# Folding the first two chunks of a down product: seven block products for eight

## The reference, cut to what matters

```
D_MODEL = 1024; D_FF = 2816
def _swiglu(h, w_in, w_out):
    a, b = jnp.split(h @ w_in, 2, axis=-1)
    return (jax.nn.silu(a) * b) @ w_out          # "up" product, then "down" product
...
xl = xl + ml[5] * _swiglu(_modulate(_rmsnorm(xl, norm_g[l, 1]), ml[3], ml[4]), w_ffn_in[l], w_ffn_out[l])
xc = xc + mc[5] * _swiglu(_modulate(_rmsnorm(xc, norm_g[l, 1]), mc[3], mc[4]), w_ffn_in[l], w_ffn_out[l])
```

## Time and profile before

| what | us |
|---|---|
| median of three runs (lowest, highest) | 3171.95 (3167.01, 3172.81) |
| the profiled execution, device time | 3168.27 |
| its span in the trace | 3166.2 |
| TensorE busy in the span | 3006.0 |
| VectorE busy in the span | 1620.0 |
| down product of layer 0, from and to (its last latent step) | 1281.45 to 1435.55 |

### The profile page before, as it was taken

How to read it: one execution, slowest core, us unless ns; L and a number is a source line. 1 busy time by engine, 2 the same in 40 slices (tenths; PEclk the granted TensorE clock), 3 DMA queues, 4 the chain that set the end, 5 groups by cost and what they waited for, 6 DMA issues and landing times. The chain is left out here.

```text
span 3166.2 us, 33940 instructions
## 1 busy us (share of the span) xinstructions
PE 3006.0 (95%) x12718; PEld 2115.9 (67%) x12718; DVE 1620.0 (51%) x3605; ACT 815.2 (26%) x1892; POOL 351.5 (11%) x391
## 2 busy tenths in 40 slices
PE   8999999999999999998999999999999999988776
PEld 3666556758888888586776678888888744443222
DVE  3233454367773676413234447624226587777774
ACT  2222244321002100012122440010023354544443
POOL 0000000010000000100000000000000254433442
PEclk9999999999999999999999999999999999999999
DMA  6212111144442454643322224479533799999997
GB/s 242 87 60 66 54 54 53 54 148 137 125 136 67 147 156 132 205 138 107 107 76 65 73 93 157 148 256 319 197 117 96 268 415 420 420 421 420 420 417 316
DMA packets 280913, 584.86 MB, mean 185 GB/s; under 512 B 11752, under 2 KB 231784, under 8 KB 244400
## 3 DMA queue, kind: packets, MB, share of 16 engines
q0 software_dynamic: 51504, 338.98, 27.2%
q1 hardware_dynamic: 229248, 243.73, 23.9%
HBM read 581.58 MB, written 1.08 MB: 184 GB/s over the span
## 5 line engine op out<-in xcount | busy, mean ns | idle before, releaser
L815 PE MATMUL banks<-normed,weight_ring 128*128 128x512 f32 (+1 forms) x1280 | 484.4, 533 | 12.8 <-PEq L322 12.4
L815 PEld LDWEIGHTS banks<-normed,weight_ring 128*128 128x128 f32 x1280 | 242.7, 191 | 232.7 <-issue 221.8
L824 PE MATMUL banks<-weight_ring,normed 128*128 128x256 f32 x1408 | 318.8, 381 | 0.0
L3710 PE MATMUL banks<-weight_ring,work 128*128 128x512 f32 x512 | 251.7, 616 | 55.1 <-ACT work L3572 54.0
L824 PEld LDWEIGHTS banks<-weight_ring,normed 128*128 128x128 f32 x1408 | 263.8, 190 | 53.5 <-issue 19.4
L3710 PE MATMUL banks<-work 128*128 128x512 f32 x512 | 251.1, 613 | 41.0 <-ACT work L3572 38.8
L436 DVE CUSTOM_DVE_ANT_0 work<-work 128x1024 f32<-128x1024 f32 x176 | 209.2, 1223 | 114.4 <-DMA work<-ada_turned 52.6
L2164 PE MATMUL banks<-normed,weight_ring 128*128 128x256 f32 x1088 | 239.0, 383 | 6.6 <-ACT normed L2364 3.8
L2164 PEld LDWEIGHTS banks<-normed,weight_ring 128*128 128x128 f32 x1088 | 208.9, 192 | 36.2 <-ACT normed L2364 4.2
L1660 PE MATMUL banks<-branches,weight_ring 128*128 128x256 f32 (+1 forms) x656 | 209.2, 481 | 3.4 <-PEq L322 3.4
L3710 PEld LDWEIGHTS banks<-weight_ring,work 128*128 128x128 f32 x512 | 88.6, 191 | 166.3 <-ACT work L3572 102.5
(11 more groups left out here) (558 smaller groups left out, 3952.6 us busy)
## 6 DMA issues: line engine op xcount, KB each, us to landing
weight_ring<-w_in SPq DMA_DIRECT2D x98, 1024.0 KB, 5.3
weight_ring<-w_ffn_in SPq DMA_DIRECT2D x44, 1024.0 KB, 5.4
work<-ada_turned POOLq DMA_DIRECT2D x80, 512.0 KB, 3.8
work<-ada_turned POOLq DMA_DIRECT2D x16, 1536.0 KB, 9.1
weight_ring<-w_ffn_out SPq DMA_DIRECT2D x20, 1024.0 KB, 5.3
weight_ring<-w_out SPq DMA_DIRECT2D x12, 1024.0 KB, 5.4
weight_ring<-w_br_ml SPq DMA_DIRECT2D x8, 1024.0 KB, 5.2
weight_ring<-w_br_da SPq DMA_DIRECT2D x8, 1024.0 KB, 5.4
```

Source lines behind the costliest of these rows:

```text
L815: last = pe.matmul(proj_bank(tile)[:, since:T], w[:, kk, half * P:(half + 1) * P], c.h[:, kk, since:T], start=kk == 0, stop=kk == KT - 1)
L824: last = pe.matmul(proj_bank(tile)[:, x * CHUNK:(x + 1) * CHUNK], c.h[:, kk, j * P:(j + 1) * P], w[:, kk, :], start=kk == 0, stop=kk == KT ...
L3710: last = pe.matmul(c.banks[2 * t + half][:], diag[:, r, :], vrows[r][:, half * 512:(half + 1) * 512], start=e == t * H * K, stop=e == (t + ...
```

## The change

Steps 0 and 1 of the down product are computed in the folded form, over the three cuts in turn with the partial sums left in four PSUM banks. Seven times 11 matmuls of 256 tokens take the place of 44 of 512 tokens in each. VectorE gets a mixture of the weights for each of the six cuts (`mix_cut`) and mixtures of the tokens for the 11 pairs of input tiles: six pairs one at a time behind the up chunks, four pairs together and the last one behind the last up chunk. It also unfolds both products into `spare` and adds them from there (`add_folded`). The modulation tiles are dealt out anew, 5, 5, 6 and 5 between these steps; their number stays 21. The plain steps use other PSUM banks, and the squares of steps 0 and 1 are both summed behind step 2.

```diff
-    BEFORE_OUT, BEFORE_DOWN, DOWN_FIRST = 32, 59, 12
+    BEFORE_OUT, BEFORE_DOWN, DOWN_FIRST = 32, 59, 10
+    FOLDED_DOWN, EARLY_PAIRS, LATE_PAIRS = 2, 6, 4
...
-    B_OUT, B_SUMS, B_UP, B_DOWN = 0, KT, KT + 2, 4
+    B_OUT, B_SUMS, B_UP, B_DOWN = 0, KT, KT + 2, 0
...
+            def folded_down(d):
+
+                n = len(folded) + d
+                first, second, third, fourth = (c.banks[4 * (n % 2) + i] for i in range(4))
+                pe.wait_ge(c.folded_copied, n - 1)
+                for cut, (k0, nk) in enumerate(cuts):
+                    w, pairs = weights(W_DOWN + d * len(cuts) + cut)[:, 0:nk], range(k0 // 2, (k0 + nk) // 2)
+                    mixed = weight_sums[:, mixed_number(d, cut) % 2]
+                    opens, closes = cut == 0, cut == len(cuts) - 1
...
+                    pe.wait_ge(c.fed, pairs[-1] + 1)
+                    done(one(first, 0, their(0, 0), tokens(0, 0), True, True))
+                    if opens:
+                        pe.wait_ge(c.folded_read, 4 * (n - 2) + 1)
+                    one(second, 0, their(1, 0), tokens(1, 0), True, False)
+                    pe.wait_ge(c.weights_mixed, mixed_number(d, cut) + 1)
+                    pe.wait_ge(c.tokens_mixed, 4 + pairs[-1] + 1)
+                    done(one(second, 1, mixture(1), token_mixture(1), False, True))
...
+                    if not closes:
+                        last.then_inc(c.slot_used, 1)
...
+            for d in range(FOLDED_DOWN):
+                folded_down(d)
             for s, (chunk, p0, p1) in enumerate(down_steps):
+                if s < FOLDED_DOWN:
+                    continue
...
-                if s:
-                    sums(down_steps, s - 1, wide * KT, B_SUMS_2)
+                if s == FOLDED_DOWN:
+                    pe.wait_ge(c.folded_read, 4 * (len(folded) + FOLDED_DOWN))
+                    sums(down_steps, 0, wide * KT, B_SUMS_2)
+                sums(down_steps, s - 1, wide * KT, B_SUMS_2)
...
+            def mix_cut(d, cut):
+
+                m, number, nk = mixed_number(d, cut), W_DOWN + d * len(cuts) + cut, cuts[cut][1]
+                out = weight_sums[:, m % 2, :, 0:nk // 2]
+                wait_weights(dve, number)
+                w = c.ring[:, number % SLOTS, 0:nk]
+                if m - 2 < len(folded):
+                    dve.wait_ge(c.folded_product, 4 * (m - 1))
+                else:
+                    wait_cut(dve, *divmod(m - 2 - len(folded), len(cuts)))
+                chain.mark(dve.tensor_tensor(out[:, 0], part_of(w, 0, 1), part_of(w, 1, 1), ALU.add))
+                chain(dve.tensor_tensor(out[:, 2], part_of(w, 0, 0), part_of(w, 0, 1), ALU.subtract))
+                chain(dve.tensor_tensor(out[:, 1], out[:, 0], part_of(w, 0, 0), ALU.subtract))
+                chain(dve.tensor_tensor(out[:, 3], part_of(w, 1, 0), out[:, 1], ALU.subtract))
+                dve.sem_inc(c.weights_mixed, 1)
...
                 if n + 1 < len(folded):
                     mix_weights(n + 1)
+                else:
+                    mix_cut(0, 0)
                 condition(2 if i == 0 else 1)
                 unfold(n)
                 if i:
                     feed(n, chunk)
+                if i and chunk < EARLY_PAIRS:
+                    mix_tokens(ffn[:, 2 * chunk:2 * chunk + 2, :], down_sums(chunk))
+            late = EARLY_PAIRS + LATE_PAIRS
+            mix_tokens(ffn[:, 2 * EARLY_PAIRS:2 * late, :],
+                       c.work[:, SUMS_AT:SUMS_AT + LATE_PAIRS * 4 * NCTX].rearrange("p (k s t) -> p s k t", s=4, k=LATE_PAIRS),
+                       LATE_PAIRS)
+            mix_tokens(ffn[:, 2 * late:NF, :], down_sums(late))
+            mix_cut(0, 1)
 
             assert taken == BEFORE_DOWN
             scales(mod_next, KT, c.vector("norm_g", 2 * KT, 3 * KT))
-            for s in range(len(down_steps)):
-                if s < 2:
-                    condition(DOWN_FIRST if s == 0 else 9)
-                add(down_steps, s, P_DOWN, D_DOWN, B_DOWN, 5 * KT)
+            condition(5)
+            mix_cut(0, 2)
+            condition(DOWN_FIRST - 5)
+            mix_cut(1, 0)
+            unfold(len(folded))
+            add_folded(0)
+            mix_cut(1, 1)
+            condition(6)
+            mix_cut(1, 2)
+            condition(5)
+            unfold(len(folded) + 1)
+            add_folded(1)
+            for s in range(FOLDED_DOWN, len(down_steps)):
+                add(down_steps, s, P_DOWN - 2 * FOLDED_DOWN, D_DOWN, B_DOWN, 5 * KT)
...
```

More of the change, by code:

```diff
@@ L1569, in tail_of_all, with down_sums, mixed_number, wait_cut @@
     D_DOWN = wide * KT
-    B_OUT, B_SUMS, B_UP, B_DOWN = 0, KT, KT + 2, 4
+    B_OUT, B_SUMS, B_UP, B_DOWN = 0, KT, KT + 2, 0
     B_SUMS_2 = B_DOWN + KT
+    def down_sums(pair):
+        if pair < 4:
+            its = c.mg[:, 2 * pair:2 * pair + 2, :].rearrange("p k t -> p (k t)")
+        elif pair == 4:
+            its = gates[1]
+        elif pair == 5:
+            its = c.big[:, NF:NF + 2, :].rearrange("p k t -> p (k t)")
+        elif pair < EARLY_PAIRS + LATE_PAIRS:
+            at = SUMS_AT + (pair - EARLY_PAIRS) * 4 * NCTX
+            its = c.work[:, at:at + 4 * NCTX]
+        else:
+            its = c.h[:, 4:6, :].rearrange("p k t -> p (k t)")
+        return its.rearrange("p (s k t) -> p s k t", s=4, k=1)
+    def mixed_number(d, cut):
+        return len(folded) + d * len(cuts) + cut
+    def wait_cut(engine, d, cut):
+        if cut == len(cuts) - 1:
+            engine.wait_ge(c.folded_product, 4 * (len(folded) + d + 1))
+        else:
+            engine.wait_ge(c.slot_used, d * (len(cuts) - 1) + cut + 1)
     def weight_of(n):
@@ L1598, in target_of @@
     def target_of(n):
+        if n >= len(folded):
+            return spare
         kind, i, chunk = folded[n]
@@ L1635, in wait_used @@
                     s, _, cut = down[n - W_DOWN]
-                    if cut == len(cuts) - 1:
-                        sp.wait_ge(c.product, P_DOWN + 2 * (s + 1))
+                    if s < FOLDED_DOWN:
+                        wait_cut(sp, s, cut)
+                    elif cut == len(cuts) - 1:
+                        sp.wait_ge(c.product, P_DOWN + 2 * (s - FOLDED_DOWN + 1))
                     else:
@@ L1713, in folded_product, with one, their, mixture @@
                 one(fourth, 1, their(1, 1), token_mixture(3)).then_inc(c.folded_product, 1)
+            def folded_down(d):
[6 more added lines that the diff above has]
+                    opens, closes = cut == 0, cut == len(cuts) - 1
+                    def one(out, half, left, right, first_of_bank, last_of_bank):
+                        for k, pair in enumerate(pairs):
+                            last = pe.matmul(out[:, half * NCTX:(half + 1) * NCTX], left(k), right(pair),
+                                             start=opens and first_of_bank and k == 0,
+                                             stop=closes and last_of_bank and k == len(pairs) - 1)
+                        return last
+                    def their(inputs, outputs):
+                        return lambda k: part_of(w, inputs, outputs)[:, k]
+                    def mixture(i):
+                        return lambda k: mixed[:, i, k]
+                    def tokens(inputs, half):
+                        return lambda pair: quarter(ffn, 2 * pair + inputs, half)
+                    def token_mixture(i):
+                        return lambda pair: down_sums(pair)[:, i, 0]
+                    def done(last):
+                        if closes:
+                            last.then_inc(c.folded_product, 1)
+                    pe.wait_ge(c.fed, pairs[-1] + 1)
[6 more added lines that the diff above has]
+                    done(one(second, 1, mixture(1), token_mixture(1), False, True))
+                    if opens:
+                        pe.wait_ge(c.folded_read, 4 * (n - 2) + 3)
+                    one(third, 0, mixture(0), token_mixture(0), True, False)
+                    done(one(third, 1, mixture(2), token_mixture(2), False, True))
+                    if opens:
+                        pe.wait_ge(c.folded_read, 4 * (n - 2) + 4)
+                    one(fourth, 0, mixture(3), tokens(1, 1), True, False)
+                    last = one(fourth, 1, their(1, 1), token_mixture(3), False, True)
+                    done(last)
+                    if not closes:
+                        last.then_inc(c.slot_used, 1)
@@ L1776, in _ @@
                         if cut == 0 and p0 == 0:
-                            pe.wait_ge(c.folded_read, 4 * (len(folded) - (2 if t < 4 else 1) + 1))
+                            pe.wait_ge(c.folded_read, 4 * (len(folded) + 1))
                         elif cut == 0:
@@ L1803, in condition, with mix_tokens @@
                     next(conditioning)
-            def mix_tokens(source, out):
+            def mix_tokens(source, out, count=1):
                 def half(inputs, tokens):
@@ L1813, in mix_tokens @@
```

(13 more changed lines are left out.)

4 lines of the change are left out of this document (2 added, 2 removed).

## The result

The changed kernel takes 3180.72 us (median of 10 runs, 3174.83 to 3185.56), the kernel before 3172.36 us (10 runs, 3167.01 to 3180.21). The ratio is 1.0023, with a 95% interval of 1.0012 to 1.0033, so the change costs about 7.3 us (8.4 by the two medians). The forecast was 3174.8, within 0.2% of no change, and that did not come true: 3180.72 lies above the 3178.3 that the forecast had set as the border to slower. It is inside the range by 0.3 us only, where rival B had put it (3180.6).

A forecast was written before the change was run, and what follows sets the result against it. TensorE bounds the kernel, but would wait for VectorE's mixtures behind modulation tiles: -9.0 + 1.8 + 7.4 + 1.8 + 0.8 = +2.8 us on the median 3171.95, giving 3174.8 us; range 3166.0 to 3181.0.

The forecast's parts named there:

- rival B: Down product: the three tile groups come at their worst, 14.4 + 15.3 + 18.4 us; +8.7 us, 3180.6; chance 0.16.
- matmuls saved: TensorE, down steps 0 and 1: 77 folded matmuls take 33.25 instead of 37.77 us per chunk; -9.0 us for both.
- wait for (0,2): TensorE in chunk 0 asks for this cut's weight mixture at 1308.2, ready at 1310.0; 1.8 us.
- wait for (1,0): TensorE at chunk 1's first cut asks for its mixture at 1319.9, ready at 1327.3; 7.4 us.
- slow clock behind it: TensorE at 1.2 GHz after a long gap: 1.8 us extra behind the wait for (1,0), none behind the wait for (1,2).
- wait for (1,2): TensorE at chunk 1's last cut asks for its mixture at 1352.5, ready at 1353.3; 0.8 us.
- The work beside the up chunks: VectorE's small token mixtures and the mixture of cut (0,0), covered by its waits for TensorE; priced at nothing.
- The first two groups of tiles: VectorE, five modulation tiles each ahead of cuts (0,2) and (1,0): 14.0 us (bounds 12.0, 14.4) and 14.4 (12.0 to 15.3).
- The third group: VectorE, six modulation tiles ahead of the mixture of cut (1,2): 15.8 us (14.25 to 18.4), weight load at its third tile.
- The mixture of (1,1): VectorE's weight mixture for a cut of 8 k in chunk 1: four operations of 0.69 us, 2.75 us in all.
- The clock's price: TensorE's lower level of 1.2 GHz after gaps of 2.28 us or more: about 1.8 us extra; nearly none after 1.82 us.
- The turns of the DMA queues: Equal turns would make a tile load behind a weight load take 5.0 us, not 6.15; sum then about -0.7 us.

The follow-up runs named there:

- the run with tiles late: Changed kernel with VectorE making each mixture as early as possible and nine modulation tiles moved behind the add of chunk 1; 3164.03 us, ratio 0.9975 against the kernel before.
- the control: The changed kernel run once more, nothing altered, beside the kernel before on the same chip; 3181.45 against 3172.28 us, ratio 1.0033.
- the probe: Kernel before, TensorE made to wait for VectorE ahead of steps 2 to 5; 0.1 us extra behind gaps of 1.29 and 2.57 us, total time not used.
- the run with small loads: Changed kernel in its own order, 20 of 21 tile loads of the down product cut to 64 of 1024 columns; 3162.52 us, a single run.

## Why the prediction was right and wrong

The forecast had the mechanism, the place of each gap and their order, and was too low by 5.7 us in the profile. Step by step, in us:

| step | forecast | changed kernel |
|---|---|---|
| matmuls saved | -9.0 | -9.06 (the run with tiles late) |
| wait for (0,2) | 1.8 | 1.98 |
| wait for (1,0) | 7.4 | 7.05 |
| slow clock behind it | 1.8 | 2.9 |
| wait for (1,2) | 0.8 | 3.25 |
| slow clock behind it | 0 | 1.75 |
| drain at three gaps | 0 | 0.5 |
| sum | +2.8 | +8.4 (measured +8.47) |

**The work beside the up chunks** was priced at nothing, rightly. The stage times don't show it, since they begin behind it; the timeline of TensorE does: from 700 us to the first matmul of the down product it is busy without a gap in both kernels (581.45 of 581.45 us before, 584.20 of 584.20 in the changed kernel).

**The first two groups of tiles** were taken at 14.0 and 14.4 us and took 13.9 and 14.0. Reading them as groups from the trace of before, collision included, worked.

**The third group** is the term that was mis-sized: 15.8 us forecast, 18.2 measured (17.2 in the control, from 1340.98 to 1358.21). Its bound of 18.4, tiles 13 to 18 of before, was nearer, though not the same case: there GpSimd's pair adds at 1320.83 held a tile load back by about 0.8 us, to 1322.98, while here they were over before the group began. The weight load fell on the load of the fourth tile, not on the third. The forecast's own times put it there too: cut (1,0) ends at 1337.8, and the fourth tile's load is issued some 3.1 us after the group begins at 1335.3.

```profile
1342.09 0.37 SPq L1678 DMA_DIRECT2D weight_ring<-w_ffn_out  x1
```

```profile
1335.79 1.90 POOL L2175 TENSOR_TENSOR normed<-normed 128x256 f32<-128x256 f32 x2 [7.63 <-ACT normed L2111]
...
1342.31 0.53 POOL L406 DMA_DIRECT2D work<-ada_turned  x1 [0.92 <-DVEq L442]
```

The load issued at 1342.31 was usable at 1350.99, 8.7 us later, not the 6.15 that I had taken from the earlier trace rows as the worst.

**The mixture of (1,1)** took 3.7 us (1335.29 to 1338.97) in place of 2.75. Two of its operations ran 1.22 and 1.09 us instead of 0.69 while GpSimd's pair add at 1335.79 was at work. The forecast counted pair adds for the sums of squares only, not beside a mixture. Every run of the folded form shows the same two long operations; the mixtures of 512 elements with no pair add beside them keep 0.69 us.

These two, less the 1.1 us by which the longer slow stretch held TensorE itself back, put the third wait at 3.25 instead of 0.8 us, which carried it over the point where the clock has a price. Rival B had that course: it said gaps of 2.2, 8.4 and 3.5 us and +8.7. But B took all three groups at their worst, and only the third one was. That its sum is so near is partly luck: the second gap was 1.35 us shorter than B's and the two slow stretches together 1.05 us longer. That the range held the result is luck too, since it ended at B's time. B's chance of 0.16 was too low, since one bad group and a pair add beside a mixture were enough for its outcome.

**The clock's price** was taken as 1.8 us for every gap of 2.28 us or more. The size is not one number: 1.6 to 3.2 us in the nine cases of these runs. The lower point was off as well inside a run of dense matmuls: 2.57 us cost nothing in the probe, though 2.28 us did at the start of another stage. That row was no match: ahead of its gap TensorE ran small matmuls, and the granted clock was already 0.68 from 2328 to 2331 us.

**The turns of the DMA queues.** The Trainium skill, "DMA: Bandwidth & Descriptors", Queues, rings and completion order, says that each DMA engine takes turns between its queues, packet by packet. I read from it that a small load would slip in between the packets of a weight load. Where both queues have packets, the trace agrees: from 1345 to 1350 us of the changed kernel the tile loads (q0, GpSimd's queue) and the weight load (q1, SyncE's) move side by side. The columns are packets, MB and the time that the packets took, as a share of 16 engines' time:

```profile
q0 software_dynamic: 240, 0.88, 47.8%
q1 hardware_dynamic: 618, 0.62, 39.8%
```

The delay stands ahead of that. By the packet records, the first packet of a lone load comes 1.23 us (0.5 MB, issued at 1285.62 in the kernel before) or 1.25 us (32 KB, issued at 1301.94 in the run with small loads) after its issue. Behind a weight load it comes 3.58 us after the issue at 1296.42 and 2.52 us after the issue at 1330.19. In between, only the weight load moves: q1 is the one queue with packets from 1296.8 to 1299.9 in the kernel before, and from 1330.2 to 1332.4 in the run with small loads:

```profile
q1 hardware_dynamic: 918, 0.94, 91.7%
```

```profile
q1 hardware_dynamic: 803, 0.82, 107.7%
```

For the load of 0.5 MB this is the whole 2.35 us: from its first packet to its landing it takes as long as the lone one. For the small load it is 1.27 of the 3.03 us, and another 1.4 us pass between the last two of its 16 landings (1333.83 and 1335.22). So the reading by turns priced a part of the load that was not the slow one. What keeps the first packet back, no run here shows.

**Still open.** The run-to-run spread of the changed kernel (3174.83 to 3185.56) is wider than these causes show in two profiles. The third gap, with its own length and the clock's price behind it, explains some 3 us of it; the rest isn't settled.

## What to carry to other kernels

When an engine that had slack becomes the maker of operands, give it a schedule by due times: here each mixture's due time is a fixed number of matmuls after the cut begins, and work that waits for DMA belongs behind it, not in front. Sum an in-order engine's row with its DMA waits in, group by group, and take each group from the stretch of the trace that has the same neighbours. Leave room even then: the third group took 18.2 and 17.2 us in two profiles of the same kernel. Seven block products for eight saved nothing until the row was reordered; the reordering turned +0.23% into -0.25%.

## What the hardware showed that I had not expected

A VectorE operation with two inputs in SBUF slows down beside a GpSimd add: 1.22 and 1.09 us against 0.69 for 512 elements, and the two adds take 1.90 against 1.40 us. It can fall on GpSimd alone: in the kernel before the tile at 1320.54 kept its 1.23 us, and the two pair adds beside it took 2.21. The Trainium skill, "GPSIMD Engine Reference", 1. Specifications, says that the two engines share their SBUF interfaces and get in each other's way when VectorE has two SBUF inputs; the trace agrees, with the numbers just given.

A tile load of 32 KB is held up by a 1 MB load of another queue as one of 0.5 MB is: it took 5.05 us in one case and 3.40 in another, where alone it takes 2.02; for 0.5 MB it was 6.15 and 8.7 us against 3.80. In three of these cases the first packet came 2.34 (the 3.40 one), 2.52 (the 5.05 one) and 3.58 us (the 6.15 one) after the issue, instead of 1.25.

TensorE's slow stretch behind a gap costs about the same for a gap of 3.8 and of 9.3 us, 1.6 and 1.9 us, but 3.2 us behind one of 2.96; the granted clock is 0.50 in each of these stretches.
